# The transposed half of a block-doubling inverse: turned with the identity, in place of a second set of join products

## The reference

```python
def step(state, inp):
    r_t, w_t, k_t, v_t, kk_t, a_t = inp
    sa = jnp.einsum('bhvk,bhk->bhv', state, -kk_t)
    state = (state * w_t[:, :, None, :]
             + sa[..., None] * (kk_t * a_t)[:, :, None, :]
             + v_t[..., None] * k_t[:, :, None, :])
    return state, jnp.einsum('bhvk,bhk->bhv', state, r_t)
```

## Time and profile before

| what | us |
|---|---|
| median of 3 runs | 863.99 (862.10, 864.23, 863.99) |
| the profiled execution | 862.3 |
| its span, first to last instruction | 860.5 |
| PE busy in the span | 845.9 (98%) |
| DVE busy | 541.4 (63%) |
| ACT busy | 394.3 (46%) |
| DMA, mean rate | 163 GB/s |
| gate stage, from 94.7 to about 194.6 us of the span | 99.9 |

### The profile page before, as it was taken

The page is one execution under the profiler, slowest core; times in us unless marked ns, Lnnn a source line. Parts: engine busy times, 40 slices in busy tenths (PEclk is TensorE's granted clock), DMA queues, the critical chain, the costliest instruction groups (busy, mean ns, idle before and its releaser), DMA issues.

```text
span 860.5 us, 16646 instructions
## 1 busy us (share of the span) xinstructions
PE 845.9 (98%) x7306; PEld 778.8 (91%) x7306; DVE 541.4 (63%) x597; ACT 394.3 (46%) x464; POOL 4.6 (1%) x7
## 2 busy tenths in 40 slices
PE   9999999999999999999999999999999999999997
PEld 8999889898989999999999999988898899999996
DVE  5998754545887655555558555586654765665564
ACT  7552333175377443434357343455544543444432
POOL 0000100000000000000000000000000000000000
PEclk9999999999999999999999999999999999999999
DMA  9846413321673665566544753336433465555541
GB/s 302 278 144 196 148 54 98 100 71 67 252 227 123 203 212 173 171 193 197 195 148 131 241 160 122 132 109 234 158 134 105 141 210 185 192 182 182 181 138 49
DMA packets 96747, 140.62 MB, mean 163 GB/s; under 512 B 2480, under 2 KB 79408, under 8 KB 96688
## 3 DMA queue, kind: packets, MB, share of 16 engines
q1 hardware_dynamic: 96400, 139.62, 49.3%
q10 hardware_dynamic: 288, 0.13, 0.1%
HBM read 138.69 MB, written 1.05 MB: 162 GB/s over the span
## 4 chain that ended last, share of the span: by engine, by line
PE 91%; DVE 4%; ACT 3%; issue 1%; DMA 1%; DVEq 0%; SPq 0%; ACTq 0%
PE PS L415 89%; DVE wlo L1581 2%; ACT xh L1167 1%; ACT whi L1167 1%; PE PS L520 1%; DMA xres<-in_x_dram 1%; DVE xl L1612 0%; DVE Gm L1741 0%; ACT st L1167 0%; PE PS L649 0%; PE PS L1004 0%; DVE xn L2129 0%; ACT junk L1167 0%; PE PS L1083 0%; DVE sbol L1849 0%
## 5 line engine op out<-in xcount | busy, mean ns | idle before, releaser
L1581 DVE TENSOR_TENSOR wlo<-raw,whi 128x2048 fp32r<-128x2048 f32 x124 | 283.4, 2290 | 152.4 <-ACT whi L1167 152.3
L415 PE MATMUL PS<-xh,whi 128*128 128x256 f32 x1136 | 323.5, 286 | 3.3 <-DVE wlo L1581 2.0
L415 PE MATMUL PS<-xh,wlo 128*128 128x256 f32 x1136 | 319.9, 283 | 0.0
L415 PE MATMUL PS<-xl,whi 128*128 128x256 f32 x1136 | 316.3, 283 | 0.0
L1167 ACT ACTIVATE whi<-raw 128x2048 fp32r<-128x2048 f32 (+1 forms) x130 | 240.9, 1857 | 161.3 <-PE PS L415 160.9
L415 PEld LDWEIGHTS PS<-xh,whi 128*128 128x128 f32 x1136 | 217.7, 192 | 9.8 <-issue 3.7
L415 PEld LDWEIGHTS PS<-xh,wlo 128*128 128x128 f32 x1136 | 217.8, 192 | 0.0
L415 PEld LDWEIGHTS PS<-xl,whi 128*128 128x128 f32 x1136 | 215.5, 192 | 0.9
L415 PE MATMUL PS<-whi,fh 128*128 128x512 f32 x216 | 84.4, 391 | 0.0
L415 PE MATMUL PS<-wlo,fh 128*128 128x512 f32 x216 | 84.3, 390 | 0.0
L415 PE MATMUL PS<-whi,fl 128*128 128x512 f32 x216 | 84.0, 389 | 0.0
(11 more groups left out here) (307 smaller groups left out, 1063.9 us busy)
## 6 DMA issues: line engine op xcount, KB each, us to landing
raw<-in_w_in_dram SPq DMA_DIRECT2D x32, 1024.0 KB, 5.4
raw<-in_w_up_dram SPq DMA_DIRECT2D x16, 1024.0 KB, 5.3
raw<-in_w_down_dram SPq DMA_DIRECT2D x16, 1024.0 KB, 5.0
raw<-in_w_ffn_gate_dram SPq DMA_DIRECT2D x11, 1024.0 KB, 5.4
raw<-in_w_ffn_up_dram SPq DMA_DIRECT2D x11, 1024.0 KB, 5.4
raw<-in_w_ffn_down_dram SPq DMA_DIRECT2D x11, 1024.0 KB, 5.1
raw<-in_w_kv_mem_dram SPq DMA_DIRECT2D x8, 1024.0 KB, 5.3
raw<-in_w_o_dram SPq DMA_DIRECT2D x4, 1024.0 KB, 8.1
```

What stands on the lines that cost most here:

```text
L415: return nc.tensor.matmul(o, l, r, start=start, stop=stop, **kw)
L1581: V.tensor_tensor(wlo[u % RING][:], raw[u % RING][:], whi[u % RING][:].bitcast(f32), ALU.subtract) \
```

## The change

The second set of joins goes at every level. The new columns of `TT` come instead from a transposition of the new `Tm`: `turned(v)`, 32 products of 32 columns with weights `Tm` and a part of the identity moving, in the order of `TURN`. It stands one level later, at the head of `lower(v + 1)`; DVE copies its result into `TT` at the head of `lower_out(v + 1)`. The first set of joins now runs at v = 5 as well. `lower` takes only the 32 columns of `Tm` that the level needs, so DVE masks 128x256 in place of 128x512. `amid(6)` is `turned(5)` alone, and `lower_out` also runs at i = 6.

To make room in banks 2 and 3, other work moves: `AK`'s products go from `before(2)` to `before(1)` and to banks 6 and 7; `v_tok` is turned in two parts of 4 products behind levels 2 and 3, into bank 7; `AV` goes ahead of unit 6 and `WT` behind it; `U0` goes ahead of unit 7 and `k_tok`'s products into its middle.

```diff
             def lower(v):
+                n = HD // 2
                 pe.wait_ge(sem("t_ready"), v)
-                pe.wait_ge(sem("tt_ready"), v)
-                for c, tt, s_, h, b, l, r in out_of(lambda c, tt, s_: XT[half(c), c ^ tt, s_, :], lambda c, tt, s_: Tm[half(c), c ^ tt, s_, :]):
-                    last = mm(PS[h, b * 512 + s_ * HD:b * 512 + (s_ + 1) * HD], l, r, True, True)
+                if v == 1:
+                    pe.wait_ge(sem("tt_ready"), 1)
+                else:
+                    turned(v - 1)
+                if v == 6:
+                    return
+                for c, tt, s_, h, b, l, r in out_of(lambda c, tt, s_: XT[half(c), c ^ tt, s_, :],
+                                                    lambda c, tt, s_: halves(Tm[half(c), c ^ tt, s_, :], v, 0)):
+                    last = mm(PS[h, b * 512 + s_ * n:b * 512 + (s_ + 1) * n], l, r, True, True)
                 last.then_inc(sem("g_mm"), 1)
+            def turned(v):
+                n = HD // 2
+                for c, tt, s_, h, b, l, r in out_of(lambda c, tt, s_: Tm[half(c), c ^ tt, s_, :],
+                                                    lambda c, tt, s_: halves(C("ident")[half(c), half(c)], v, 1)):
+                    last = mm(PS[h, b * 512 + 256 + s_ * n:b * 512 + 256 + (s_ + 1) * n], l, r, True, True)
+                last.then_inc(sem("turn_mm"), 1)
 
             def join(v):
                 pe.wait_ge(sem("g_ready"), v)
+                pe.wait_ge(sem("tt_ready"), v)
                 n = HD // 2
-                if v < 5:
-                    for c, tt, s_, h, b, l, r in back_to(...
-                    last.then_inc(sem("joins"), 1)
-                for tt in range(NT):
-                    if tt == 1 and v < 5:
-                        pe.wait_ge(sem("joins"), v)
-                    for s_ in range(NH):
-                        for c in range(2):
-                            g = half(c ^ tt)
-                            o = (2 + c) * 512 + 256 + s_ * n
-                            last = mm(PS[g, o:o + n], Gm[g, c, s_, :], halves(TT[g, c, s_, :], v, 1), True, True)
+                for c, tt, s_, h, b, l, r in back_to(lambda c, tt, s_: TT[half(c ^ tt), c, s_, :],
+                                                     lambda c, tt, s_: halves(Gm[half(c ^ tt), c, s_, :], v, 0)):
+                    last = mm(PS[h, b * 512 + s_ * n:b * 512 + (s_ + 1) * n], l, r, True, True)
                 last.then_inc(sem("join_mm"), 1)
...
+                    if i in (2, 3):
+                        pe.wait_ge(sem("pair_ready"), 4)
+                        pe.wait_ge(sem("tok_ready"), i - 1)
+                        for j in range(NPAIR):
+                            last = nc.tensor.transpose(PS[:, 7 * 512 + j * P:7 * 512 + (j + 1) * P],
+                                                       rw[:, 8 + j, (i - 2) * P:(i - 1) * P], C("ident"))
+                        last.then_inc(sem("tok_T"), 1)
...
             def lower_out(v):
-                dve.wait_ge(sem("g_mm"), v)
-                m = M(f"level{2 ** v}").unsqueeze(1).broadcast_to([P, NH, HD])
+                n = 2 ** v
+                if v < 6:
+                    dve.wait_ge(sem("g_mm"), v)
+                if v > 1:
+                    dve.wait_ge(sem("turn_mm"), v - 1)
+                    for x in range(2):
+                        last = V.tensor_copy(halves(TT[:, x].rearrange("p s t -> p (s t)"), v - 1, 1),
+                                             bank(2 + x)[:, 256:512].rearrange("p (a b) -> p a b", b=2 ** (v - 1)))
+                    last.then_inc(sem("tt_ready"), 1)
+                if v == 6:
+                    return
...
                 for x in range(2):
-                    last = V.tensor_tensor(Gm[:, x], bank(2 + x).rearrange("p (s t) -> p s t", s=NH), m, ALU.mult)
+                    last = V.tensor_tensor(Gm[:, x].rearrange("p s (a b) -> p s a b", b=2 * n)[:, :, :, 0:n],
+                                           bank(2 + x)[:, 0:256].rearrange("p (s a b) -> p s a b", s=NH, b=n), m, ALU.mult)
                 last.then_inc(sem("g_ready"), 1)
```

More of the change, by code:

```diff
@@ new lines, in before @@
+                if i == 6:
+                    pe.wait_ge(sem("t_ready"), 6)
+                    for c, tt, s_, h, b, l, r in out_of(lambda c, tt, s_: AK[half(c), c ^ tt, s_, :],
+                                                        lambda c, tt, s_: vt_[half(c), tt, head(slot_head(s_))]):
+                        last = mm(PS[h, b * 512 + s_ * HD:b * 512 + (s_ + 1) * HD], l, r, True, True)
+                    last.then_inc(sem("chunk_mm"), 1)
+                if i == 7:
+                    pe.wait_ge(sem("chunk_ready"), 2)
+                    for c, tt, s_, h, b, l, r in back_to(lambda c, tt, s_: TT[half(c ^ tt), c, s_, :], lambda c, tt, s_: AV[half(c ^ tt), c, s_, :]):
+                        last = mm(PS[h, b * 512 + s_ * HD:b * 512 + (s_ + 1) * HD], l, r, True, True)
+                    last.then_inc(sem("chunk_mm"), 1)
@@ new lines, in amid @@
+            def amid(i):
+                if i == 0:
+                    pe.wait_ge(sem("sv_ready"), 2)
+                    pe.wait_ge(sem("rw_pre"), 1)
+                    pairs(kk, eX, "pair_mm")
+                    pairs(kk, eX, "pair_mm", 6, True)
+                elif i < 6:
+                    if i == 1:
+                        pe.wait_ge(sem("tok_ready"), 1)
+                    lower(i)
+                elif i == 6:
+                    pe.wait_ge(sem("chunk_ready"), 1)
+                    lower(6)
+                else:
+                    pe.wait_ge(sem("chunk_ready"), 3)
+                    tokens(eN, 0, "tok_T")
+                    pe.wait_ge(sem("sb_arg_read"), NPAIR)
+                    pairs(eN, eP, "pair_mm", 4)
@@ new lines, in behind @@
+            def behind(i):
+                if i == 0:
+                    pe.wait_ge(sem("pair_ready"), 1)
+                    pairs(eX, kk, "pair_mm")
+                elif i < 6:
+                    join(i)
+                    if i in (2, 3):
[5 more added lines that the diff above has]
+                        last.then_inc(sem("tok_T"), 1)
+                elif i == 6:
@@ L733, in before @@
                     last.then_inc(sem("chunk_mm"), 1)
[L734 to L758, removed]
-                else:
[L760 to L776, removed]
+                else:
+                    pe.wait_ge(sem("tok_ready"), 4)
                     tokens(kk, 0, "tok_T")
@@ L811, in _ @@
                 pe.wait_ge(sem("sb_w"), p_ + 1)
+                if p_ == 0:
+                    pe.wait_ge(sem("pair_ready"), 4)
+                if p_ == 2:
+                    pe.wait_ge(sem("tok_ready"), 3)
                 ob = (6 + p_ // 2) * 512 + p_ % 2 * SEQ
@@ L1309, in bank_pair, with values_tile @@
                 last.then_inc(sem(done), 1)
+            def values_tile(tt):
+                act.wait_ge(sem("tok_T"), 2 + tt)
+                A_(vt_[:, tt, :], bank(7), ACT.Copy).then_inc(sem("tok_ready"), 1)
             def gate_sigmoid(c):
@@ L1341, in _ @@
                 hi(U_G[2 * p_] + RING)
+                if p_ == 1:
+                    values_tile(1)
                 if p_ == 3:
+                    bank_pair(kt_, "tok_T", 4, "tok_ready")
                     nc.scalar.preload_act_table_set("sigmoid_and_others")
@@ L1736, in lower_out @@
             def lower_out(v):
-                dve.wait_ge(sem("g_mm"), v)
-                m = M(f"level{2 ** v}").unsqueeze(1).broadcast_to([P, NH, HD])
+                n = 2 ** v
[9 more added lines that the diff above has]
+                    return
+                m = M(f"level{n}").rearrange("p (a b) -> p a b", b=2 * n)[:, :, 0:n].unsqueeze(1).broadcast_to([P, NH, HD // (2 * n), n])
                 for x in range(2):
-                    last = V.tensor_tensor(Gm[:, x], bank(2 + x).rearrange("p (s t) -> p s t", s=NH), m, ALU.mult)
+                    last = V.tensor_tensor(Gm[:, x].rearrange("p s (a b) -> p s a b", b=2 * n)[:, :, :, 0:n],
+                                           bank(2 + x)[:, 0:256].rearrange("p (s a b) -> p s a b", s=NH, b=n), m, ALU.mult)
                 last.then_inc(sem("g_ready"), 1)
             def joined(v):
[L1746 to L1749, removed]
                 dve.wait_ge(sem("join_mm"), v)
[L1752 to L1755, removed]
                 for x in range(2):
-                    last = add(TT, x, 1)
-                last.then_inc(sem("tt_ready"), 1)
+                    part = halves(Tm[:, x].rearrange("p s t -> p (s t)"), v, 0)
+                    last = V.tensor_tensor(part, part, bank(2 + x)[:, 0:256].rearrange("p (a b) -> p a b", b=2 ** v), ALU.add)
+                last.then_inc(sem("t_ready"), 1)
             def gate_unit(i):
@@ L1763, in gate_unit @@
                     lo(U_G[i - 1] + RING)
-                if 0 < i < 6:
+                if 0 < i < 7:
                     lower_out(i)
@@ L1767, in gate_unit @@
```

(2 more changed lines are left out.)

27 lines of the change are left out of this document (6 added, 21 removed).

## The result

The changed kernel takes 856.95 us (median of 4 runs, 855.36 to 857.37) against 863.05 (4 runs, 862.04 to 864.23) for the kernel before: ratio 0.9925, 95% interval 0.9904 to 0.9947. That is 6.1 us less at the medians. A second comparison gave 857.07 against 863.66, ratio 0.9928 (0.9912 to 0.9945). The forecast was 855.4 with a range of 852.3 to 859.0. One run of the kernel before, in the comparison with the later experiments, took 1668 us and is in none of the ratios.

The account below looks back on a forecast made before the run. PE was taken as the bound, busy 845.9 of 860.5 us. Savings of 4.90 + 0.70 + 0.72 + 1.54 = 7.86 put the profiled 862.3 at 854.4; weighing the median's 854.4 or 856.1 gave 855.4, range 852.3 to 859.0.

Parts of the forecast that it names:

- the quadrants: Gate stage joins on PE: 32 products take 1.98 us alternating between two quadrants, 0.95 in four.
- sum of 7.86: Whole kernel: 4.90 for products, 0.70 for waits, 0.72 for a standstill, 1.54 for the clock, all us less.
- rival 1: Only the products count; clock fall and issue hole recur elsewhere: 5.60 us less, 856.7 to 858.4; chance 0.22.
- Second sets gone for `turned`: Gate stage on PE: five second sets of joins go, 9.90 us; `turned` five times comes, 4.75.
- Net 4.90 on PE: Gate stage products: 9.90 and 0.70 (narrower `lower`) saved, 4.75 (`turned`) and 0.95 (level 5 joins) added.
- The rule that was weighed there and set aside: For `lower`: a one-column product has the latency of 60, so halving columns saves nothing; 4.20 us instead of 4.90.
- The moved products cost the same: `AK`, `v_tok`, `AV`, `WT`, `U0`, `k_tok` on PE keep number and shape, so no cost change at new places.
- Waits 0.70 less: PE waits for DVE in the gate stage: 1.26 us for `Gm` goes, 0.55 comes at levels 4, 2 and unit 6.
- The end of the stage: `b_tok` on ACT comes later, but some 0.2 of 0.5 us slack remains: no wait, 0.3 at worst.
- 0.72 for the hole: PE's standstill amid `AK`'s products, marked "issue", taken as gone: 0.72 us less, with 0 as other end.
- 1.54 for the clock: The granted clock's fall at 157.70, behind level 4's wait and joins, taken as gone: 1.54 us less, or 0.
- Rival 4: Slower: clock falls after each stretch of small products, 1.54 us each; at ten +9.1 us, 873 by median; chance 0.03.

Follow-up runs that it names:

- two_quadrants: Changed kernel with the 32 products of `turned` issued two quadrants at a time, same operands: 859.88 us against 857.07 for the changed kernel.
- second_twice: Kernel before, with the second set of joins made twice at every level: 880.31 us against 863.55, ratio 1.0205.
- after_again: Changed kernel, unchanged, run again for a second trace: 857.07 us against 863.66 for the kernel before, ratio 0.9928.
- turned_twice: Changed kernel with `turned` made twice at every level: 863.19 us, ratio 1.0000 to the kernel before.
- ak_moved: Kernel before, with only AK's products moved ahead of unit 1, to banks 6 and 7, and masked in unit 1: ratio 1.0001.

## Why the prediction was right, and where not

It was right in sign and in its main mechanism, the quadrants: 855.4 forecast, 856.95 measured, in the range. But its sum of 7.86 is not how the 6.1 came about, and 856.95 also lies in the range of rival 1 (856.7 to 858.4), which describes the stage better. That the forecast is only 1.6 off is in part luck: terms of 1.2, 0.7 and 1.5 us did not come as it reasoned, and waits of 0.4 and a lower number of falls made up for some of it. By its own steps:

1. **Second sets gone for `turned`.** Right: `turned` holds PE for 0.95 us, in four quadrants, where the removed sets held it for 1.98 in two. `two_quadrants` and `second_twice` show that it is the quadrants.
2. **Net 4.90 on PE.** Mis-sized. It took 0.95 for a set at any place and gave the 0.14 more in `lower` to the columns. A level from 2 to 4 costs 4.02 before and 0.95 + 1.05 + 1.06 = 3.06 after, 0.96 less. Level 1 goes from 4.02 to 2.14, level 5 stays at 3.07, and `turned(5)` alone in unit 6 costs 1.07. Sum: 3 x 0.96 + 1.88 - 1.07 = 3.69. The 1.2 us that lack are 0.5 of the 0.7 that it gave to the columns of `lower`, and 0.7 for the passages to other products, which the five first sets of joins and `turned(5)` now pay. The rule that was weighed there and set aside would have given 4.20, nearer.
3. **The moved products cost the same.** Wrong by 0.27 us, though their number and shape are kept. `v_tok` in two parts of four takes 1.09 where it took 0.79, and `k_tok` in the middle of unit 7 takes 0.97 where it took 0.79; their neighbours give 0.2 back.
4. **Waits 0.70 less.** New ones: 0.15, 0.1 and 0.3 forecast, 0.14, 0.13 and 0.21 measured. Those that went were more than the brackets showed: 1.62 by starts against 1.26. Net 1.14. A bracket counts from a group's modelled end, so small waits drop out of it.
5. **The end of the stage.** Right: 0.2 us of slack forecast, 0.15 left.
6. **0.72 for the hole.** Wrong step: it was taken as belonging to the old order. It is at the same place in three traces of the old order (0.72, 0.36, 0.68), but holes of 1.45 and 0.61 stand in two of the five traces of the new order (`after_again`, `turned_twice`), and `ak_moved`, without a hole, gained nothing. In the first pair of traces it counts in full (AK's products went from 2.08 to 1.09); what it is worth on the mean, so few traces don't tell.
7. **1.54 for the clock.** Wrong step: "both things that stand ahead of the fall shrink" took the fall of one trace for an effect of what stood ahead of it. The unchanged kernel showed it elsewhere the next time, with the same wait and the same joins ahead. The change does go with fewer falls, but that is worth some 1.1 us (6.1 less 5.0), and not for the reason given.

Rival 4 has a slip: ten falls instead of the one are nine more, 13.9 less the 6.32 saved, so 7.5 us slower and not 9.1. It decides nothing.

For the first pair of traces the stage closes: 3.69 - 0.27 + 1.14 + 0.99 (hole) + 1.36 + 0.26 (fall) = 7.17, measured 7.19. Without hole and fall 4.6 is left; the second pair, less the 1.68 and 0.63 that its holes cost, gives 4.8, and the times at equal clock 5.0. So the likeliest single account is rival 1, only the products and waits count: 5.6 there, 4.6 to 5.0 by these rows.

## What to carry to other kernels

Count small fp32 products by quadrant. In this kernel 64 records in two quadrants took 1.87 us, so two records in the same 64x64 quadrant stand 58 ns apart, with 32 columns and hardly more with 64; 32 products take 0.93 us in four quadrants and 1.87 in two. Here a transposition that reaches the idle quadrants was worth the 32 products more that it needs. Price a set with what follows it: the last one in a row pays 0.11 us for the passage to other shapes, and going from 64 to 32 columns saves 0.02. And before a stall or a fall of the clock enters a sum, look whether a second trace of the same kernel has it at the same place.

## What the runs showed of the hardware that I had not expected

A set in two quadrants overlaps with the next set in the others, though both are in one queue: `lower` starts while the last products of `turned` still go, and a set costs 0.72 us more than in four quadrants instead of 0.93.

The granted clock fell to 0.50 (1.2 GHz) between 63 and 66 us in four of the ten traces, while PE was busy all the time in the records, and 16 to 17 us behind the end of the gate stage (from 206 to 211 us, and at 226.6 in the longer `second_twice`) in five. Each of these nine falls begins within 1.5 us after the end of the products with 8 rows; the other traces have the same products there and no fall. In `second_twice`, with 3.85 us of joins in two quadrants at each level and holes of 1.48, 1.12 and 1.28 us, it fell in the stage twice, the first time for twice as long as anywhere else:

```profile
120.90:127.50 6.60, 5.90 (x97) 4.73 (x97) 1.42 (x4) 1.59 (x2) 0.00 (x0) 0.50 0.01 2
141.40:144.70 3.30, 3.30 (x10) 2.10 (x9) 1.18 (x4) 0.00 (x0) 0.00 (x0) 0.50 0.02 5
```

The first begins within the hole of 1.48, the second 0.9 us behind the one of 1.12. So doubling the sparse work costs 9.3 us by its products and, with the holes and falls that come with it, 17. The changed kernel, with less of this work, has fewer falls; whether that is the reason for 1.1 of its 6.1 us stays open.
